# The last three items of an expert sweep: two by one-hot products, one by an indirect add, the second copy by accumulating loads

## The reference

```python
def step(y, blk):
    tok, gate, e = blk
    xb = x_pad[tok]
    h = jax.nn.silu(xb @ w_gate[e]) * (xb @ w_up[e])
    out = (h @ w_down[e]) * gate[:, None]
    return y.at[tok].add(out), None
...
h = h + (routed + shared).reshape(bsz, s, d)
return rms_norm(h, final_norm_g)
```

## Time and profile before

| | us |
|---|---|
| median of 3 runs (1288.5 to 1291.15) | 1290.93 |
| the profiled execution, its own time | 1289.51 |
| its span, first to last instruction | 1287.8 |
| TensorE busy in the span | 1261.3 (98%) |
| VectorE, ScalarE, GpSimd busy | 854.6, 773.9, 457.4 |
| the loop's last down product ends | 1257.1 |
| the last of the one-hot products ends | 1278.0 |
| the last store lands | 1287.8 |

### The profile page before, as it was taken

One profiled execution on the slowest core, in us unless ns is written; L12 is line 12 of the kernel. 1 busy time (PEld: TensorE's weight loads), 2 busy tenths in 40 slices (PEclk: granted clock), 3 DMA queues, 4 the chain that ended last, 5 costly groups with the idle time before them and its releaser, 6 DMA issues.

```text
span 1287.8 us, 27241 instructions
## 1 busy us (share of the span) xinstructions
PE 1261.3 (98%) x6219; PEld 1050.0 (82%) x6220; DVE 854.6 (66%) x1222; ACT 773.9 (60%) x1087; POOL 457.4 (36%) x600
## 2 busy tenths in 40 slices
PE   7999999999999999999999999999999999999996
PEld 6888787888787888888888888888888888888885
DVE  5222564468956777767767677678677687677767
ACT  6222083233456777767777677677777676777763
POOL 1322141000023444444444444444444444444463
PEclk9999999999999999999999999999999999999999
DMA  9120262211458999999999999999999999999988
GB/s 335 34 70 1 114 244 79 85 72 68 164 212 313 321 340 326 316 307 332 326 331 315 325 335 335 331 327 337 342 325 312 318 359 298 340 317 323 346 251 248
DMA packets 81269, 337.21 MB, mean 262 GB/s; under 512 B 12752, under 2 KB 15952, under 8 KB 64592
## 3 DMA queue, kind: packets, MB, share of 16 engines
q1 hardware_dynamic: 53872, 250.73, 50.6%
q0 software_dynamic: 27360, 86.01, 27.4%
HBM read 288.14 MB, written 65.27 MB: 274 GB/s over the span
## 4 chain that ended last, share of the span: by engine, by line
PE 95%; DVE 2%; ACT 1%; DMA 1%; issue 0%; POOLq 0%; POOL 0%; SPq 0%; ACTq 0%; DVEq 0%
PE ps L850 39%; PE ps_out L864 20%; PE ps L524 10%; PE ps L506 7%; PE ps L654 6%; PE ps L711 4%; PE ps L872 2%; PE ps L906 1%; PE ps_out L693 1%; PE ps L602 1%; PE ps_out L739 1%; PE ps L739 1%; DMA w_in_sb<-in_w_in 0%; DMA y_rows_dram<-ob 0%; PE ps_out L906 0%
## 5 line engine op out<-in xcount | busy, mean ns | idle before, releaser
L850 PE MATMUL ps<-w_gu,xTh 128*128 x1488 | 468.0, 396 | 1.8 <-DVE xTl L1711 1.8
L1510 DVE TENSOR_TENSOR w_gu<-raw_gu,w_gu (+1 forms) x256 | 296.6, 1220 | 71.7 <-ACT w_gu L1174 71.7
L850 PEld LDWEIGHTS ps<-w_gu,xTh 128*128 128x128 f32 x1488 | 273.0, 188 | 56.3 <-issue 2.8
L850 PE MATMUL ps<-w_gu,xTl 128*128 x744 | 291.5, 392 | 0.0
L1174 ACT ACTIVATE w_gu<-raw_gu (+1 forms) x256 | 250.0, 1049 | 1.3 <-issue 1.3
L864 PE MATMUL ps_out<-w_dn,hTh 128*128 x744 | 241.4, 406 | 0.0
L1920 POOL DMA_INDIRECT y_rows_dram<-ob,idxs x90 | 146.3, 1625 | 141.7 <-ACT ob L1197 134.6
L1517 DVE TENSOR_TENSOR w_dn<-raw_dn,w_dn (+1 forms) x128 | 151.2, 1222 | 26.8 <-ACT w_dn L1178 25.6
L850 PEld LDWEIGHTS ps<-w_gu,xTl 128*128 128x128 f32 x744 | 139.7, 188 | 29.1
L864 PEld LDWEIGHTS ps_out<-w_dn,hTh 128*128 128x128 f32 x744 | 133.3, 189 | 25.9 <-issue 0.2
L864 PE MATMUL ps_out<-w_dn,hTl 128*128 x372 | 146.5, 394 | 0.0
(11 more groups left out here) (293 smaller groups left out, 1692.3 us busy)
## 6 DMA issues: line engine op xcount, KB each, us to landing
raw_gu<-in_w_gate SPq DMA_DIRECT2D x64, 1024.0 KB, 7.5
raw_gu<-in_w_up SPq DMA_DIRECT2D x64, 1024.0 KB, 11.5
raw_dn<-in_w_down SPq DMA_DIRECT2D x64, 1024.0 KB, 13.0
x_ring<-in_x SPq DMA_DIRECT2D x8, 512.0 KB, 3.9
w_in_sb<-in_w_in SPq DMA_DIRECT2D x8, 512.0 KB, 9.6
xh<-in_x SPq DMA_DIRECT2D x8, 512.0 KB, 8.1
w_out_sb<-in_w_out SPq DMA_DIRECT2D x1, 4096.0 KB, 21.9
hn_rows_dram<-rows SPq DMA_DIRECT2D x8, 512.0 KB, 2.6
```

What stands on the lines that cost most here:

```text
L850: mm = pe.matmul(ps[3][:, :], x_[:, k, :], w_gu[:, bass.ds(at, 1), part, :, k, :], start=(k == 0 and part == 0 and x_ is xTh), stop=(k == ...
L1510: dv.tensor_tensor(gu_part(w_gu[:, :, 1, :, :, :], at, m), gu_part(raw_gu, at, m), gu_part(w_gu[:, :, 0, :, :, :], at, m).bitcast(F32), AL ...
```

## The change

Three things are changed, all in the last turn. Item `first` (u = 0) gets no one-hot matrix; its rows are added to the second copy in DRAM by one more indirect DMA, and TensorE's products are made for items 1 and 2 alone. All eight chunks of the second copy are now loaded by GpSimd's queue with addition, after that DMA has landed. And for chunks 0, 2 and 4 (`BY_GPSIMD`) ScalarE multiplies by the inverse root and GpSimd by the weight row, in place of VectorE's one instruction.

```diff
@@ sync: the loads of yb_in go, the stores wait for either engine
-            sp.wait_ge(s_hd, NE * KF)
-            sp.sem_inc(s_turn_sp, 1)
-            sp.wait_ge(s_ld, NE * KF)
-            sp.sem_inc(s_turn_sp, 1)
-            for c in range(2):
-                sp.dma_start(yb_in[:, c, :], yv2[c]).then_inc(s_x[c], 16)
             for c in range(NC):
-                sp.wait_ge(s_of, c + 1)
+                if c in BY_GPSIMD:
+                    sp.wait_ge(s_og, BY_GPSIMD.index(c) + 1)
+                else:
+                    sp.wait_ge(s_of, c + 1 - sum(g < c for g in BY_GPSIMD))
                 sp.dma_start(out_v[c], ya_in[:, c, :]).then_inc(s_ost, 16)
@@ tensor
-            pe.wait_ge(s_oh, 1)
+            down(last, *expert(last))
+            pe.wait_ge(s_oh, 2)
             pe.wait_ge(s_obh, 1)
             pe.wait_ge(s_obl, 1)
-            last_rows(0, (0,))
-            last_rows(1, (0,))
-            down(last, *expert(last))
-            pe.wait_ge(s_oh, TURN)
-            pe.wait_ge(s_obh, TURN - 1)
-            pe.wait_ge(s_obl, TURN - 1)
-            last_rows(0, (1,))
-            last_rows(1, (1,))
-            pe.wait_ge(s_obh, TURN)
-            pe.wait_ge(s_obl, TURN)
-            last_rows(0, (TURN - 1,))
-            last_rows(1, (TURN - 1,))
-            for c in range(2, NC):
+            for c in range(3):
+                last_rows(c, (1,))
+            pe.wait_ge(s_obh, 2)
+            pe.wait_ge(s_obl, 2)
+            for c in range(3):
+                last_rows(c, (2,))
+            for c in range(3, NC):
                 if c >= 4:
                     pe.wait_ge(s_sum, c - 3)
-                last_rows(c, range(TURN))
+                last_rows(c, (1, 2))
@@ scalar
-                    act.wait_ge(s_oa, i - 1)
-                    act.activation(ob_high[:, 0, :], ob[:, 0, :], ACT.Copy).then_inc(s_obh, 1)
...
+            def scaled(c):
+
+                act.wait_ge(s_rf, c + 1)
+                act.activation(ya_in[:, c, :], ya_in[:, c, :], ACT.Copy, scale=rs[:, 4, c:c + 1]).then_inc(s_scaled, 1)
+
             for c in range(NC):
                 act.wait_ge(s_sum, c + 1)
                 act.wait_ge(s_sq2, NC) if c == 0 else act.wait_ge(s_sqf, c)
                 square(ya_in[:, c, :], D ** -0.5, 4, c, s_sqf)
+                if c - 1 in BY_GPSIMD:
+                    scaled(c - 1)
@@ vector
-                    rest_ob(0)
...
-            both_copies(0)
             add_last(0)
-            both_copies(1)
             add_last(1)
             dv.wait_ge(s_gf, 32)
             for c in range(NC):
                 if c + 2 < NC:
                     add_last(c + 2)
+                if c in BY_GPSIMD:
+                    continue
                 dv.wait_ge(s_rf, c + 1)
@@ gpsimd
             gp.wait_ge(s_ga[0], gathers * 16 + 16)
-            rows_of(0)
             rows_of(1)
+            n = last_turn(gp)
+            gp.wait_ge(s_add[0], n * 16)
+            gp.sem_inc(s_turn, 1)
+            gp.tensor_copy(idxs[:, 0:1], idx_all[:, bass.ds(first, 1)]).then_inc(s_col, 1)
+            gp.wait_ge(s_col, 2)
+            gp.tensor_scalar(idxs[:, 0:1], idxs[:, 0:1], float(ROWS), None, ALU.add).then_inc(s_sc_col, 1)
+            gp.wait_ge(s_sc_col, first + 1)
+            gp.sem_inc(s_turn, 1)
+            gp.wait_ge(s_oa, first + 1)
+            gp.sem_inc(s_turn, 1)
+            for u in (1, 2):
+                n = last_turn(gp)
+                gp.wait_ge(s_add[u], n * 16)
+                gp.sem_inc(s_turn, 1)
+            gp.indirect_dma_start(out=y_d[:, :], out_offset=bass.IndirectOffsetOnAxis(ap=idxs[:, 0:1], axis=0),
+                                  in_=ob[:, 0, :], in_offset=None, compute_op=ALU.add,
+                                  bounds_check=top_dump).then_inc(s_add[0], 16)
             keep_gate(first + 2, 2)
             rows_of(2)
-            for c in range(2, NC):
+            n = last_turn(gp)
+            gp.wait_ge(s_add[0], n * 16 + 16)
+            gp.sem_inc(s_turn, 1)
+            for c in range(NC):
                 gp.wait_ge(s_x[c], 48)
-                if c == 2:
-                    for u in range(TURN):
-                        n = last_turn(gp)
-                        gp.wait_ge(s_add[u], n * 16)
-                        gp.sem_inc(s_turn, 1)
                 gp.dma_start(ya_in[:, c, :], yv2[c], accum_op=ALU.add).then_inc(s_yl[c], 16)
+            gp.wait_ge(s_gf, 32)
             for c in range(NC):
                 rstd(4, c, s_sqf, s_rf)
+                if c - 1 in BY_GPSIMD:
+                    gp.wait_ge(s_scaled, BY_GPSIMD.index(c - 1) + 1)
+                    gp.tensor_tensor(ya_in[:, c - 1, :], ya_in[:, c - 1, :], gf_row[:, :], ALU.mult).then_inc(s_og, 1)
```

More of the change, by code:

```diff
@@ L233, in build @@
                    place("ob_rest2", [P, D], F32R, T_AT)]
-        yb_in = place("yb_in", [P, 2, D], F32, Z_AT)
         tok_row = place("tok_row", [P, S], F16, M_AT + KB)
@@ L294, in build @@
         s_hg, s_lg, s_hd, s_ld, s_hl = (sem(n) for n in ("gu_high", "gu_rest", "down_high", "down_rest", "hT_rest"))
-        s_yl = {c: sem(f"y_last_in{c}") for c in range(2, NC)}
+        s_yl = {c: sem(f"y_last_in{c}") for c in range(NC)}
         s_oh, s_obh, s_obl = sem("onehot_ready"), sem("last_results_high"), sem("last_results_rest")
         s_tok, s_col = sem("token_row"), sem("last_slot_columns")
-        s_both = sem("copies_summed")
+        s_scaled, s_og = sem("sums_scaled"), sem("out_rows_by_gpsimd")
         s_lastmm, s_sum = sem("last_rows_done"), sem("last_rows_added")
@@ L906, in last_rows @@
                             mm = pe.matmul(ps[bank][:, :], onehot[u][:, c * P:(c + 1) * P],
-                                           ob_[:, half * 512:(half + 1) * 512], start=(u == 0 and part == 0),
+                                           ob_[:, half * 512:(half + 1) * 512], start=(u == 1 and part == 0),
                                            stop=(u == TURN - 1 and part == 1))
@@ L1725, in rest_ob @@
             def rest_ob(u):
-                dv.wait_ge(s_obh, u + 1)
+                dv.wait_ge(s_obh, u)
                 dv.tensor_tensor(ob_rest[u][:, :], ob[:, u, :], ob_high[:, u, :].bitcast(F32), ALU.subtract).then_inc(s_obl, 1)
@@ L1770, in _ @@
             rest_ob(1)
-            dv.wait_ge(s_obh, TURN)
+            dv.wait_ge(s_obh, 2)
             dv.tensor_tensor(ob_rest[TURN - 1][:, :], ps_out[:, :], ob_high[:, TURN - 1, :].bitcast(F32),
                              ALU.subtract).then_inc(s_obl, 1)
-            def both_copies(c):
-                dv.wait_ge(s_x[c], 64)
-                dv.tensor_tensor(ya_in[:, c, :], ya_in[:, c, :], yb_in[:, c, :], ALU.add).then_inc(s_both, 1)
             def add_last(c):
-                if c < 2:
-                    dv.wait_ge(s_both, c + 1)
-                else:
-                    dv.wait_ge(s_yl[c], 16)
+                dv.wait_ge(s_yl[c], 16)
                 dv.wait_ge(s_lastmm, c + 1)
@@ L1963, in rows_of @@
                 gp.tensor_copy(slot_col[:, u:u + 1], idx_all[:, bass.ds(first + u, 1)]).then_inc(s_col, 1)
-                gp.wait_ge(s_col, u + 1)
+                gp.wait_ge(s_col, 2 * u - 1)
                 gp.tensor_scalar(onehot[u][:, :], tok_row[:, :], slot_col[:, u:u + 1], None, ALU.is_equal).then_inc(s_oh, 1)
@@ L1970, in _ @@
             gp.wait_ge(s_ga[0], gathers * 16 + 16)
-            rows_of(0)
             rows_of(1)
+            n = last_turn(gp)
[15 more added lines that the diff above has]
+                                  bounds_check=top_dump).then_inc(s_add[0], 16)
             keep_gate(first + 2, 2)
             rows_of(2)
-            for c in range(2, NC):
+            n = last_turn(gp)
+            gp.wait_ge(s_add[0], n * 16 + 16)
+            gp.sem_inc(s_turn, 1)
+            for c in range(NC):
                 gp.wait_ge(s_x[c], 48)
-                if c == 2:
-                    for u in range(TURN):
-                        n = last_turn(gp)
-                        gp.wait_ge(s_add[u], n * 16)
-                        gp.sem_inc(s_turn, 1)
                 gp.dma_start(ya_in[:, c, :], yv2[c], accum_op=ALU.add).then_inc(s_yl[c], 16)
+            gp.wait_ge(s_gf, 32)
             for c in range(NC):
                 rstd(4, c, s_sqf, s_rf)
+                if c - 1 in BY_GPSIMD:
+                    gp.wait_ge(s_scaled, BY_GPSIMD.index(c - 1) + 1)
+                    gp.tensor_tensor(ya_in[:, c - 1, :], ya_in[:, c - 1, :], gf_row[:, :], ALU.mult).then_inc(s_og, 1)
 BUTTERFLY = 18
+BY_GPSIMD = (0, 2, 4)
 TERMS_AFTER = [12, 14, 15, 18, 16]
```

## The result

| | before | changed |
|---|---|---|
| median of five runs, us | 1289.46 | 1296.82 |
| lowest to highest, us | 1288.5 to 1291.15 | 1296.05 to 1297.76 |
| span of the profiled execution, us | 1287.8 | 1295.1 |

The ratio is 1.0057 with a 95% interval of 1.0046 to 1.0068: the changed kernel is slower, by 7.4 us. The forecast was slower by 3.5 us (1294.4 us), with a range up to 1298.0. It was counted from 1290.93, the median of three of the five runs before; from 1289.46 the same 3.5 us give 1293.0.

The account below looks back on a forecast made before the run. TensorE bounds the kernel before, q0's accumulating loads the changed one: chunk 7 lands at 1261.4 + 18.1 + 2.0 = 1281.5 instead of 1278.04, +3.5 us with the tail unchanged. From 1290.93 that gives 1294.4 us, range 1290.5 to 1298.0.

Parts of the forecast that it names:

- slack of 2.1 us: Kernel before: the second copy's last load lands at 1275.9, 2.1 us ahead of its need at 1278.04.
- TensorE's 7.4 us: Item 0's 32 one-hot matmuls removed, 0.230 us each: 7.4 us won, all spent waiting for q0.
- The stream of loads: Accumulating loads after chunk 0's: seven at 2.58 us, 18.1 us, plus 2.0 us for the stores' share.
- The first landing: Chunk 0's accumulating load: issued at 1255.4, landing 6.0 us later at 1261.4.
- The tail: Behind the last add for chunk 7: square, inverse root, scaling, store; 9.8 us, expected unchanged.
- with two register loads more I take 1246.2: GpSimd's issue of the extra indirect add, behind the wait for `ob` of item 0, finished at 1245.15.
- the choice of 9 us between 6.0 and 10.4: Extra add's issue to landing, beside 4.2 MB of plain loads: 9 us, landing at 1255.2.
- The engines' budget: DMA engines' work: 28.2 us before, 33.4 us changed, 5.2 more, of which 2.1 are slack.
- starves: Extra add waits until q1's plain loads are out, landing at 1257.6; +5.9 us, 1296.8 us; chance 0.17.
- beside the adds: GpSimd's three scaling products, 2.6 us each (at most 4.4), fit beside VectorE's adds.
- Faster: q0 is not the bound; eight loads land at the plain rate, 10.2 us; -6.5 us, 1284.4 us; chance 0.13.
- little changes: Add lands after 6.0 us, loads start at 1256.7, stores overlap little; +1.1 us, 1292.0 us; chance 0.22.

Follow-up runs that it names:

- e11: Kernel before with all eight second-copy chunks by accumulating loads, scaling all on VectorE, no extra add; 1291.90 us, ratio 1.0018.
- e1: Kernel before with all eight second-copy chunks by accumulating loads and GpSimd scaling chunks 0, 2 and 4, no extra add; 1291.49 us, ratio 1.0020.
- e3: Changed kernel without the extra indirect add and the wait for it, item 0's rows left out of the output; 1291.39 us, ratio 1.0019.
- e6: Changed kernel with SyncE's plain loads of the first copy's chunks 4 to 7 held back until the extra add has landed; 1297.94 us, ratio 1.0064.
- e2: Changed kernel with no scaling on GpSimd, VectorE scaling all eight chunks; 1296.94 us, ratio 1.0058.
- e10: Kernel before with only GpSimd's and ScalarE's scaling of chunks 0, 2 and 4 added; 1291.33 us, ratio 1.0015.
- e4: Changed kernel with second-copy loads plain on GpSimd's queue, overwriting the first copy, whose values the output lacks; 1292.74 us, ratio 1.0028.
- e5: As e4, but VectorE scales all eight chunks; 1290.51 us, ratio 1.0004.

## Why the prediction came out as it did

**Direction and bound: right.** The bound moved from TensorE to q0's accumulating transfers, and the slack of 2.1 us was used up by the two extra accumulated chunks alone (e11). TensorE's 7.4 us were worth nothing (e1 against e3). It was through at 1275.9 and not by 1274, since it waited 2.65 us for VectorE and then ran at the lower clock for 3.4 us; nothing waited for it. The size was not right: 7.4 us against 3.5. That the time is 2.4 us above the 1294.4 and not 3.9 is owed to the slower median that the forecast was counted from.

**The stream of loads: right in sum, in part by luck.** From the first add to the last I forecast 18.1 + 2.0 = 20.1 us; it was 1285.11 - 1264.98 = 20.1 us. The first five intervals were 12.4 us and not 12.9, so a load took 2.49 us and not 2.58, 17.4 for seven. The stores cost 7.70 - 2 x 2.49 = 2.7 us in the last two intervals and nothing before, since none of their packets moved before 1277.3. The two differences cancel.

**The first landing: mis-sized, by 4.2 us.** This is the whole miss. Counted from the start of the first one-hot matrix:

| step | forecast | measured | off |
|---|---|---|---|
| start of the matrix to the add's issue | 6.6 | 8.1 | +1.5 |
| the add's issue to landing | 9 | 10.96 | +2.0 |
| landing to the first load's issue | 0.2 | 0.62 | +0.4 |
| that issue to VectorE's first add | 6.0 | 6.29 | +0.3 |

The tail is 0.2 longer, and the loop was 0.6 shorter: 4.2 + 0.2 - 0.6 = 3.8, which is 7.3 of span measured less the 3.5 forecast.

The first line is the step "with two register loads more I take 1246.2". `ob` was out at 1243.51 + 1.02 = 1244.53 and the issue came 2.6 us behind, not 1.05. Two more groups of a register load and its semaphore steps stand between the wait for `ob` and the add; in the chain of this execution the first two of three such groups take 1.0 and 0.7 us (1244.65 to 1246.34), and I had given the two more 0.15 us together. The second is the choice of 9 us between 6.0 and 10.4; the measured value lies outside the bounds that I took from three rows. None of those three adds was issued 5 us into 4.2 MB of plain loads, as this one was. e6 holds half of these back and lands in 7.2 us, so it is what stands on q1 that sets most of this time.

**The engines' budget: the amount was right, the idle time was missing.** I let the first load meet engines that are free "by about 1256.7" and took the 6 us of a lone transfer behind its issue. That lone 6 us begins with 2.2 us in which nothing of it moves (1236.70 to 1238.87). Here the first packet came 1.7 us behind the issue, at 1260.4, and this time lay bare, with the wait for the semaphore ahead of it. The dependent transfer left a hole in the bound resource; the budget of 33.4 us has no line for it. (The lower end of the landing's effect, -1.3, is -1.0 by the prediction's own figures: 1260.4 against 1261.4.)

**The rival "starves": its number, not its mechanism.** It gave 1296.8 us, and 1296.82 was measured. It said that q0 gets nothing until q1 is through. For the first 5.9 us this was so, but then the two shared (1253 to 1257), and the add's late issue and the idle time made up the difference. That the number fits is luck. e6 shows starving of this kind for 4 us on the loads themselves. What decides whether the queues share is not settled by these runs. In both stretches of starving q0 had nothing moving when q1's loads were waiting. The same is seen the other way round: the first store moved no packet for 3.8 us while q0 had the engines (1273.50 to 1277.3), and 3.6 us before (1267.34 to 1271.0), where SyncE's first load on free engines took 1.0 us in the changed kernel (1242.35 to 1243.35). So in these stretches the queue that comes second waits, whichever it is; that is an observation, and nothing was tried on it.

**GpSimd's scaling "beside the adds": right here, wrong as a general price.** e2 shows nothing. The reason was that VectorE and the roots had time; where they have none it costs 1.9 (e10) and 2.2 us (e4 against e5).

**"Faster" and "little changes": refuted.** Plain loads on q0 reach 418 GB/s (e4), accumulating ones kept to 209 over the 11 us from 1266 to 1277, where no store stood beside them.

## What to carry to other kernels

Count the work of the DMA engines in time, not in bytes: an accumulating transfer cost two plain ones, so engines that look half free by GB/s are full, and unloading TensorE onto them can lose more than it saves. A transfer that must wait for another one's landing costs its bytes (2.4 us here) and besides the hole between the two (3.1 us), from the semaphore over the issue to the first packet. Before a part is handed from VectorE to GpSimd, look at what stands behind it in GpSimd's order, and at whether the two can run at the same time at all.

## What was unexpected of the hardware

TensorE's granted clock fell in the changed kernel. PE had been idle for 2.65 us before 1266.33, waiting for VectorE to free its banks. The stretches behind it, in the columns of the windows above:

```profile
1267.00:1269.00 2.00, 2.00 (x7) 1.51 (x6) 1.29 (x2) 0.66 (x3) 0.79 (x2) 0.51 1.02 203
...
1271.00:1273.00 2.00, 2.00 (x10) 1.65 (x9) 0.89 (x2) 1.15 (x2) 1.94 (x1) 1.00 1.02 201
```

From 1267 to 1269 the clock is at 0.51, the lower level of 1.2 GHz, and a matmul of 512 columns comes every 0.43 us instead of 0.23; by 1271 it is back at 1.00. TensorE was not the bound there, so it cost nothing. In e4, where PE waited 1.19 us at this place, the clock stayed at 1.00.

That GpSimd's transfers stood back behind SyncE's for some 4 us (e6), SyncE's stores behind GpSimd's loads for 3.8, and that they shared elsewhere, I had not expected in this size either.
